# Sigmoids of the recurrent heads as exp(-ln(1+exp(-x))) on ScalarE, with activation table sets loaded by name

## The reference, cut to what matters

```python
va = jax.nn.silu(heads(ia, H_A))                 # ia * sigmoid(ia)
oa, S = gla_scan(heads(qa, H_A), ka, va, logf, s0)
oa = head_rms_norm(oa, gn.reshape(H_A, 1, DV_A))
oa = ... oa * jax.nn.sigmoid(ga)
...
def rms_norm(x, g):
    y = x32 * lax.rsqrt(jnp.mean(x32 * x32, axis=-1, keepdims=True) + EPS)
```

## Time and profile before

| | |
|---|---|
| time, median of 3 runs | 3168.53 us (3167.55 to 3171.75) |
| span of the profiled execution | 3168.7 us, 70413 instructions |
| PE busy | 2880.0 us (91%) |
| DVE busy | 2161.4 us (68%) |
| ACT busy | 1500.1 us (47%) |
| `ACT_TABLE_LOAD` on ACT | 127 of 1283 ns each: 30 at line 812, 30 at 850, 8 each at 897, 900, 939, 941, 963, 996, 998, 5 each at 822 and 824, 1 at 1013 |

### The profile page before, as it was taken

The page is one execution under the profiler, slowest core; times in us unless marked ns, Lnnn a source line. Parts: engine busy times, 40 slices in busy tenths (PEclk is TensorE's granted clock), DMA queues, the critical chain, the costliest instruction groups (busy, mean ns, idle before and its releaser), DMA issues.

```text
span 3168.7 us, 70413 instructions
## 1 busy us (share of the span) xinstructions
PE 2880.0 (91%) x22723; PEld 2687.5 (85%) x22723; DVE 2161.4 (68%) x5865; ACT 1500.1 (47%) x2828; POOL 144.8 (5%) x277
## 2 busy tenths in 40 slices
PE   7888883677789999999999999999699999999997
PEld 7788872334489999999999988898599999999997
DVE  4799978766666777756756665666466677757656
ACT  4333322333256765544545444554356755545544
POOL 0111101222100000000000000000000000000000
PEclk9899986666799999999999999999799999999999
DMA  6598854676655555555555656655455565655654
GB/s 218 205 323 310 310 206 144 224 244 236 230 174 171 178 184 183 181 180 181 182 181 171 203 200 212 219 192 198 149 179 172 179 185 180 184 179 180 190 168 138
DMA packets 181550, 627.56 MB, mean 198 GB/s; under 512 B 19536, under 2 KB 40416, under 8 KB 177104
## 3 DMA queue, kind: packets, MB, share of 16 engines
q1 hardware_dynamic: 135056, 449.74, 44.5%
q0 software_dynamic: 37920, 138.97, 12.9%
q10 hardware_dynamic: 8480, 37.59, 3.3%
HBM read 597.50 MB, written 28.73 MB: 198 GB/s over the span
## 4 chain that ended last, share of the span: by engine, by line
PE 73%; DVE 16%; issue 4%; DMA 3%; ACT 2%; DVEq 1%; ACTq 0%; POOLq 0%; POOL 0%; SPq 0%
PE stream L465 22%; PE stream L466 21%; PE stream L467 21%; DVE kring L1261 5%; DVE wlo L1138 4%; DMA vring<-in_cache_v 2%; PE stream L532 1%; PE mix L564 1%; PE mix L592 1%; DVE Sb L1261 1%; PE mix L674 1%; DVE ze L1179 1%; DMA raw<-in_w_even_in 1%; ACT whi L812 0%; PE mix L681 0%
## 5 line engine op out<-in xcount | busy, mean ns | idle before, releaser
L1138 DVE TENSOR_TENSOR wlo<-raw,whi 128x512 fp32r<-128x512 f32 (+1 forms) x1696 | 1099.6, 680 | 550.0 <-ACT whi L812 538.4
L812 ACT ACTIVATE whi<-raw 128x512 fp32r<-128x512 f32 (+1 forms) x1696 | 1014.6, 620 | 952.3 <-PE stream L467 825.3
L465 PE MATMUL stream<-hA_hi,whi 128*128 128x264 f32 x2688 | 787.9, 293 | 77.1 <-DVE ze L1179 40.0
L465 PE MATMUL stream<-hB_hi,whi 128*128 128x264 f32 x2816 | 800.9, 284 | 3.8 <-DVE ab L1199 3.8
L466 PE MATMUL stream<-hB_lo,whi 128*128 128x264 f32 x2816 | 799.2, 284 | 0.0
L467 PE MATMUL stream<-hB_hi,wlo 128*128 128x264 f32 x2816 | 798.7, 284 | 0.0
L466 PE MATMUL stream<-hA_lo,whi 128*128 128x264 f32 x2688 | 775.0, 288 | 0.0
L467 PE MATMUL stream<-hA_hi,wlo 128*128 128x264 f32 x2688 | 773.8, 288 | 0.0
L465 PEld LDWEIGHTS stream<-hA_hi,whi 128*128 128x128 f32 x2688 | 519.5, 193 | 104.6 <-DVE wlo L1138 58.9
L465 PEld LDWEIGHTS stream<-hB_hi,whi 128*128 128x128 f32 x2816 | 531.7, 189 | 4.3 <-DVE wlo L1138 4.2
L466 PEld LDWEIGHTS stream<-hB_lo,whi 128*128 128x128 f32 x2816 | 532.1, 189 | 0.1
(11 more groups left out here) (320 smaller groups left out, 2715.5 us busy)
## 6 DMA issues: line engine op xcount, KB each, us to landing
raw<-in_w_f_in SPq DMA_DIRECT2D x352, 512.0 KB, 3.7
kring<-in_cache_k POOLq DMA_DIRECT2D x128, 512.0 KB, 5.2
vring<-in_cache_v POOLq DMA_DIRECT2D x128, 512.0 KB, 5.0
raw<-in_w_f_o SPq DMA_DIRECT2D x128, 512.0 KB, 3.6
raw<-in_w_odd_in SPq DMA_DIRECT2D x128, 512.0 KB, 3.8
raw<-in_w_even_in SPq DMA_DIRECT2D x112, 512.0 KB, 6.0
raw<-in_w_f_o SPq DMA_DIRECT2D x64, 384.0 KB, 3.5
raw<-in_w_even_out SPq DMA_DIRECT2D x32, 512.0 KB, 4.1
```

The lines of the kernel that those rows point to most:

```text
L465: mm(bank, hi, p.src[0][:, kt, :], start=first, stop=False)
L812: A(whi[:, 4 * j + k, 0:n], raw[:, 4 * j + k, 0:n], ACT.Copy).then_inc(hi_done, 1)
L1138: v.tensor_tensor(wlo[:, 4 * j + k, 0:n], raw[:, 4 * j + k, 0:n], whi[:, 4 * j + k, 0:n].bitcast(F32), ALU.subtract).then_inc(lo_done, 1)
```

## The change

Both sigmoids become exp(-ln(1 + exp(-x))): ACT adds four instructions per head to piece 1 (two Ln with bias 1, two Exp with scale -1), DVE drops two additions and two reciprocals. At five places of the program ACT loads a table set by name: the set that holds both Ln and Exp before each of the five model-width roots, before the recurrent stage, and in each retention head behind its Silu; the set that holds Silu in each retention head behind its rough root. The semaphore step lists of both engines follow.

```diff
+LN_EXP, SILU = "natural_log_exp_and_others", "silu_and_others"
...
             def rough_root(n):
 
+                act.preload_act_table_set(LN_EXP)
                 act.wait_ge(IV.sem, IV.at("var", n))
                 A(sq[:, :], var[:, :], ACT.Ln).then_inc(IA.sem, IA.one("ln"))
...
                     A(va[par][:, :], tile(ze, h + Z_IA), ACT.Exp, scale=-1.0).then_inc(GA.sem, GA.one("ei"))
+                    act.wait_ge(GA.sem, GA.at("eg", h))
+                    A(sg[par][:, :], sg[par][:, :], ACT.Ln, bias=1.0).then_inc(GA.sem, GA.one("lg"))
+                    act.wait_ge(GA.sem, GA.at("ei", h))
+                    A(va[par][:, :], va[par][:, :], ACT.Ln, bias=1.0).then_inc(GA.sem, GA.one("li"))
+                    act.wait_ge(GA.sem, GA.at("lg", h))
+                    A(sg[par][:, :], sg[par][:, :], ACT.Exp, scale=-1.0).then_inc(GA.sem, GA.one("sg"))
+                    act.wait_ge(GA.sem, GA.at("li", h))
+                    A(va[par][:, :], va[par][:, :], ACT.Exp, scale=-1.0).then_inc(GA.sem, GA.one("si"))
...
                     A(gate[:, :, :], zo[:, z + Z_G:z + Z_G + 2, :], ACT.Silu).then_inc(QA.sem, QA.one("silu"))
+                    act.preload_act_table_set(LN_EXP)
...
                     A(qr[:, 0, :], r1[:, :], ACT.Exp, scale=-0.5).then_inc(QA.sem, QA.one("rough"))
+                    act.preload_act_table_set(SILU)
...
             act.wait_ge(SV.sem, SV.before(1))
+            act.preload_act_table_set(LN_EXP)
             take_weights(0)
...
                 elif piece == 1:
-                    dve.wait_ge(GA.sem, GA.at("ei", h))
-                    v.tensor_scalar(sg[par][:, :], sg[par][:, :], 1.0, None, ALU.add).then_inc(GV.sem, GV.one("g1"))
-                    dve.wait_ge(GV.sem, GV.at("g1", h))
-                    v.reciprocal(sg[par][:, :], sg[par][:, :]).then_inc(GV.sem, GV.one("sg"))
-                    v.tensor_scalar(va[par][:, :], va[par][:, :], 1.0, None, ALU.add).then_inc(GV.sem, GV.one("i1"))
-                    dve.wait_ge(GV.sem, GV.at("i1", h))
-                    v.reciprocal(va[par][:, :], va[par][:, :]).then_inc(GV.sem, GV.one("ir"))
-                    dve.wait_ge(GV.sem, GV.at("ir", h))
+                    dve.wait_ge(GA.sem, GA.at("si", h))
                     v.tensor_tensor(va[par][:, :], va[par][:, :], tile(ze, h + Z_IA), ALU.mult).then_inc(GV.sem, GV.one("va"))
```

More of the change, by code:

```diff
@@ L345, in hybrid_step @@
         GV = Steps(sem("hgrn_gates_vector"),
-                   ["ls", "mxf", "g1", "sg", "i1", "ir", "va", "cum", "dk"] + [f"d{l}{s}" for l in range(LEVELS) for s in "lr"] + ["kd"])
-        GA = Steps(sem("hgrn_gates_scalar"), ["abs", "exp", "ln", "ka", "fg", "eg", "ei", "dke", "levels"])
+                   ["ls", "mxf", "va", "cum", "dk"] + [f"d{l}{s}" for l in range(LEVELS) for s in "lr"] + ["kd"])
+        GA = Steps(sem("hgrn_gates_scalar"), ["abs", "exp", "ln", "ka", "fg", "eg", "ei", "lg", "li", "sg", "si", "dke", "levels"])
         HV = Steps(sem("hgrn_vector"),
```

## The result

The changed kernel takes 3147.95 us (3142.55 to 3149.62, four runs), the kernel before in the same session 3170.07 (3167.55 to 3171.75): a ratio of 0.9932, 95% interval 0.9919 to 0.9946, so 21.5 us less (17.1 to 25.7). Against the runs of the kernel before in the later sessions (62 runs, medians 3166.7 to 3167.9) it is 19 to 20 us less. The forecast was 11.9 us less, 3156.6. The time lies in the forecast range, 0.95 us above its lower end, and that is partly luck: the lower end came from rival (e) or from five heads that are 1.9 us short, while the runs show some 6 us in the heads and some 6 behind the roots, which stood in no term and no rival. The time also lies where rival (e) had put it, at 3148, but rival (e) is not the reason, as will be seen.

The account below looks back on a forecast made before the run. PE, busy nine tenths of the span, bounds the streaming stages; in the recurrent stage whoever is last at each meeting, there the value pages. Gates 2.9, roots 6.4 and last heads 2.6 sum to 11.9 us off, 3156.6; range 3147 to 3164.

Parts of the forecast that it names:

- rival (e): At seven places on the path: a load holds ACT longer than its row; 9.0 us more, 3148; chance 0.02.
- five heads that are 1.9 us short: Recurrent heads: five going like head 5, about 1.9 us under the usual 39; an alternative basis for lower end 3147.
- The gates of head 0: Start of the recurrent stage: both reciprocals leave the chain, DVE's multiply comes at 559.47 instead of 562.39; 2.9 us.
- The five roots: Model-width roots: each loses one table load of 1.28 us between Ln and Exp; 6.4 us in all.
- The last heads: Last recurrent and last retention head: the load between Ln and Exp leaves the chain, 1.28 us each; 2.6 us.
- The retention loop's named loads: Retention heads: up to 18 new loads against 23 that go, all taken as covered; 0, bounded by 23 us.
- Rival (d): Retention loop: new loads stand between weight copies and PE runs out of weights; slower, up to 3180; chance 0.04.
- The reciprocals inside the loop: Recurrent heads: states come 4.2 us earlier, but value pages hold product o; booked 0, ends 0 and 29 us.
- Rival (a): Recurrent heads: the states hold product o after all; 0 to 29 us more gain, down to 3128; chance 0.04.
- rival (b): Recurrent heads re-phase against page fetches and granted clock, giving back 6 to 9 us; about 3163 to 3166; chance 0.18.
- The estimate of 3147: Seven loads on the path at the skill's switch price of about 2.66 us: 18.6 us, time 3147.

Follow-up runs that it names:

- the thrice one: The kernel before, with each of a recurrent head's two reciprocals taken three times on DVE; 46.6 us slower than the kernel before.
- the filled one: The changed kernel with 14 idle matmuls on PE at the end of each recurrent head; 10.8 us less than the kernel before.
- e3: The changed kernel with the store of each head's prompt state held until page 11 is used; 18.7 us less than the kernel before.
- e6: The changed kernel with three copies on ACT ahead of each root's Ln; 6.0 us less than the kernel before.
- e7: The changed kernel with one copy on ACT ahead of each root's Ln, which doesn't wait for it; 20.3 us less than the kernel before.
- e2: The kernel before with only the two sigmoids moved to ACT, no table set named; 4.4 us less than the kernel before.
- e1: The kernel before with only the named table loads, the sigmoids keeping DVE's reciprocals; 14.3 us less than the kernel before.
- the padded kernel: The same run as e6: the changed kernel with three copies ahead of each root's Ln; 6.0 us less than the kernel before.

## Why the forecast was right in kind and short in size

**The gates of head 0** (forecast 2.9): 2.88 measured, by the mechanism given, down to the spacing of 0.31 us.

**The five roots** (forecast 6.4): here the sum fell short. The term was the load's own length and nothing behind it. Root 4, behind which PE has nothing to stream, gave 1.29 (14.96 on average in the kernels without the names, 13.67 in those with them). Roots 1 to 3 gave 1.28 + 1.52 each, 8.4 in place of 3.8, and the tail of the first feed-forward another 2.4. Root 0 gave its 1.27 at PE's stall, but by the end of the attention heads it is gone: that point comes 517.3 us after root 0's Ln before and 517.8 after. So the roots and the tail give about 12.1 in place of 6.4; the kernel with the names in the roots alone measured 11.4 (7.3 to 15.2), the last recurrent head's load included. The numbers for it stood in the profile: the stalls of 1.9 us were read the earlier trace rows, the granted clock of the 4 us behind them was not. The working asked what PE waits for and not at what speed it goes on; that is the term it left at nothing.

**The last heads** (forecast 2.6): the last retention head gave 1.28 (timeline of PE, its wait was 7.55 before):

```profile
2262.18 0.58 PE L466 MATMUL stream<-mixed_hi,whi 128*128 128x264 f32 x1 [6.27 <-DVE mixed_lo L1546]
```

The last recurrent head gave about 1.3 at PE's wait for the first weights (8.35 before, 7.07 after), but the output projections of the two layers take 0.6 and 0.4 longer, for reasons not traced.

**The retention loop's named loads** (forecast 0): from root 2's Ln to PE's first tile of the odd output projection it takes 526.19 us with the names in the roots alone and 524.75 to 525.45, 525.1 on average, in the five kernels with all of them and no filler. The 1.1 us between them are about the 1.28 of the last head, so the loop's names neither gave nor cost more than about 0.5. Rival (d) had no share.

**The reciprocals inside the loop** (forecast 0, ends 0 and 29): more than 0, but far from 29. Six kernels with the reciprocals on DVE (the thrice one aside) have seven periods of 267.0 to 276.9 us, 272.5 on average; five with the new sigmoids (the filled one aside) 263.2 to 272.1, 268.5 on average. The 4 us between the averages are smaller than the spread in either group (9 to 10 us). But the scatter is the seventh period's. The first six take, in one execution of each, 226.05 to 226.22 us in the four kernels that have both halves of the change (after, e3, e6, e7), 229.91 to 233.60, 231.8 on average, in the six with the reciprocals on DVE, and 230.15 with the sigmoids alone (e2). So both halves together take about 5.7 us off six heads, and neither does so by itself: the names alone leave 233.11 (e1). The profiled execution of the changed kernel was a good draw in the seventh, 37.1 us. The same six heads as windows, before and after, columns as above:

```profile
567.88:801.36 233.48, 177.18 (x1321) 92.52 (x1321) 166.46 (x337) 80.26 (x162) 50.89 (x96) 0.68 0.71 243
565.69:791.75 226.06, 164.38 (x1321) 88.91 (x1321) 141.53 (x313) 57.59 (x162) 50.89 (x96) 0.74 0.76 250
```

PE idles 5.4 us longer there after the change and is busy 12.8 us less for the same matmuls: the gain is again in the granted clock, 0.74 for 0.68. Why it is granted more stays open. Rival (a) had the sign, but not the reason, since o waits for the states neither before nor after; rival (b) named the granted clock and had the wrong sign.

**Rival (e)**, a load that holds ACT for longer than its row, gave 3148 and the runs gave 3147.95, yet it falls: at root 4, where nothing but ACT's path counts, a load was worth 1.29 us, its row and no more; and the padded kernel lost the surplus behind roots 1 and 3 without a load. The Trainium skill, "ScalarE: Activation LUTs", section "What ACT_TABLE_LOAD costs", adds about 1380 ns of drain to a load; by it root 4 would have given 2.66, as an estimate. This case shows no such part. The estimate of 3147 that the prediction worked out from that price falls with it, near as it lies to the measured time.

**The sum again**, from the rows: gates 2.9, loads behind roots 1 to 4 3.8 + 1.3, clock behind roots 1 to 3 4.6, tail 2.4, last heads 2.6 less 1.0 given back: 16.6. The profiles outside the recurrent loop differ by 27.8 - 10.8 = 17.0. With 5.7 for the first six heads that is 22 to 23, against the measured 21.5 (17.1 to 25.7), the seventh period's scatter aside. So the forecast left out about 6 us behind the roots and about 6 us in the heads, and both are mostly time that PE got back by a higher granted clock.

## What to carry to other kernels

A stall of a busy TensorE is priced with what stands behind it: read the granted clock of the windows after the stall, beside the stall itself. A table load between Ln and Exp on the path of a reciprocal root costs its own 1.28 us, and here cost 2.8 with the clock; a set that holds both, named where the engine waits anyway, takes it off. Where an engine is late in a meeting of several (the states and the pages), measure its room by making it later, before paying for making it earlier; what earlier brings has to be measured by itself, in several executions, because one period can scatter by more than the gain.

## What the runs showed of the hardware that was not expected

Behind a stall of the table the loss was 1.70 or 1.71 us or nothing. After the stalls of 0.11 to 1.67 us there the clock was still at 1.00, after those of 1.89 to 2.40 it fell, with two exceptions: 2.03 us behind root 2 with three copies, and 2.40 at the tail with four idle matmuls behind the roots. Both have neighbours of the same length behind which it fell, so length alone doesn't decide it. Work whose result is thrown away keeps the clock as well as useful work does (four matmuls, 5.1 us gained), but only where it fits the stall: fourteen turned the gain into a loss of 5.4 us.
